# The norm between two transformer blocks: scale at the projection's eviction, raw rows transposed early, residual gain on VectorE

## The reference, cut to what matters

```python
def rms_norm(x, gain):
    xf = x.astype(jnp.float32)
    y = xf * lax.rsqrt(jnp.mean(xf * xf, axis=-1, keepdims=True) + RMS_EPS)
    return (y * gain.astype(jnp.float32)).astype(x.dtype)
...
    h = h + g2 * swiglu(u, ffn_w_gate[layer], ffn_w_up[layer], ffn_w_down[layer])
    return rms_norm(h, final_norm_g)
...
def second_block(x, mem, w_in, w_out, w_mem_kv, ln_g, ln_b, pool_w, pool_scale, w_kv_shared):
    h = x
    for i in range(DEPTH_2):
        if i == N_A_LAYERS:
            k_blocks, v_blocks, k_mean = moba_shared_kv(h, w_kv_shared)
        u = h @ w_in[i]
...
        y = mixed @ w_out[i]
        h = layer_norm(DEEPNORM_ALPHA * h + y, ln_g[i], ln_b[i])
```

## Time and profile before

| | us |
|---|---|
| three runs | 2292.22, 2295.01, 2295.14 |
| median | 2295.01 |
| profiled execution | 2295.28 |
| its span in the trace | 2293.3 |
| PE busy | 2107.2 (92%) |
| DVE busy | 1496.7 (65%) |
| ACT busy | 1062.5 (46%) |
| POOL busy | 113.0 (5%) |

### The profile page before, as it was taken

The page is one execution under the profiler, slowest core; times in us unless marked ns, Lnnn a source line. Parts: engine busy times, 40 slices in busy tenths (PEclk is TensorE's granted clock), DMA queues, the critical chain, the costliest instruction groups (busy, mean ns, idle before and its releaser), DMA issues.

```text
span 2293.3 us, 29996 instructions
## 1 busy us (share of the span) xinstructions
PE 2107.2 (92%) x9820; PEld 1732.6 (76%) x9820; DVE 1496.7 (65%) x2638; ACT 1062.5 (46%) x1931; POOL 113.0 (5%) x188
## 2 busy tenths in 40 slices
PE   5996999997889999999999999799799699999796
PEld 4775888875667887888888887588578488888675
DVE  5997998666998776655556556755245755555466
ACT  3533544464335444445544554445334354554542
POOL 2000000220003000000000000200000300000000
PEclk9998999998999999999999999899899799999998
DMA  9997999434887887666556655466426366664452
GB/s 298 357 345 264 362 365 326 122 93 158 309 296 239 270 260 250 193 191 192 186 192 192 192 189 180 137 193 194 172 90 206 91 187 195 191 196 129 169 210 99
DMA packets 321588, 486.08 MB, mean 212 GB/s; under 512 B 33696, under 2 KB 145536, under 8 KB 320064
## 3 DMA queue, kind: packets, MB, share of 16 engines
q1 hardware_dynamic: 318704, 468.63, 62.3%
q0 software_dynamic: 2768, 15.98, 2.0%
HBM read 465.13 MB, written 2.10 MB: 204 GB/s over the span
## 4 chain that ended last, share of the span: by engine, by line
PE 76%; DVE 11%; issue 6%; SPq 3%; DMA 2%; ACT 2%; POOL 0%; DVEq 0%; POOLq 0%; ACTq 0%
PE ps L468 23%; PE ps L470 23%; PE ps L469 23%; DVE w_lo L401 3%; SPq L840 3%; DVE ada_acc L413 3%; PE ps L724 1%; PE ps L687 1%; PE ps L501 1%; PE ps L671 1%; DMA raw<-in_w_mem_kv 1%; PE ps L1373 1%; ACT w_hi L368 1%; DMA raw<-in_w_out 1%; DVE evac L575 1%
## 5 line engine op out<-in xcount | busy, mean ns | idle before, releaser
L401 DVE TENSOR_TENSOR w_lo<-raw,w_hi 128x512 fp32r<-128x512 f32 (+1 forms) x1328 | 916.3, 702 | 597.7 <-ACT w_hi L368 596.0
L368 ACT ACTIVATE w_hi<-raw 128x512 fp32r<-128x512 f32 (+1 forms) x1328 | 829.5, 629 | 968.2 <-PE ps L470 911.7
L468 PE MATMUL ps<-w_hi,actT 128*128 128x512 f32 x2176 | 865.3, 398 | 55.4 <-DVE actT L582 27.4
L470 PE MATMUL ps<-w_hi,actT 128*128 128x512 f32 x2176 | 852.4, 392 | 0.0
L469 PE MATMUL ps<-w_lo,actT 128*128 128x512 f32 x2176 | 851.8, 391 | 0.0
L468 PEld LDWEIGHTS ps<-w_hi,actT 128*128 128x128 f32 x2176 | 414.1, 190 | 150.6 <-DVE actT L582 35.3
L470 PEld LDWEIGHTS ps<-w_hi,actT 128*128 128x128 f32 x2176 | 413.3, 190 | 87.2
L469 PEld LDWEIGHTS ps<-w_lo,actT 128*128 128x128 f32 x2176 | 414.7, 191 | 84.0 <-issue 1.4
L413 DVE SCALAR_TENSOR_TENSOR ada_acc<-raw,c_col,ada_acc 128x512 f32<-128x512 f32 x360 | 269.8, 749 | 10.1 <-DMA raw<-in_ada_w 2.2
L468 PE MATMUL ps<-w_hi,hidT 128*128 128x512 f32 x352 | 137.7, 391 | 2.8 <-DVE w_lo L401 2.8
L470 PE MATMUL ps<-w_hi,hidT 128*128 128x512 f32 x352 | 137.0, 389 | 0.0
(11 more groups left out here) (224 smaller groups left out, 1214.8 us busy)
## 6 DMA issues: line engine op xcount, KB each, us to landing
raw<-in_w_in SPq DMA_DIRECT2D x216, 512.0 KB, 4.3
raw<-in_ada_w SPq DMA_DIRECT2D x192, 512.0 KB, 5.7
raw<-in_w_out SPq DMA_DIRECT2D x96, 512.0 KB, 5.1
raw<-in_ffn_w_gate SPq DMA_DIRECT2D x176, 256.0 KB, 2.9
raw<-in_ffn_w_up SPq DMA_DIRECT2D x176, 256.0 KB, 3.1
raw<-in_ffn_w_down SPq DMA_DIRECT2D x88, 512.0 KB, 4.2
raw<-in_w_kv_shared SPq DMA_DIRECT2D x48, 512.0 KB, 3.6
raw<-in_w_mem_kv SPq DMA_DIRECT2D x32, 512.0 KB, 6.9
```

Source lines behind the costliest of these rows:

```text
L368: act.activation(w_hi[:, g, 0:w], raw[:, slot_of(st, it), b, 0:w], ACT.Copy).then_inc(hi_ready, 1)
L401: nc.vector.tensor_tensor(w_lo[:, g, 0:w], raw[:, slot, b, 0:w], w_hi[:, g, 0:w].bitcast(f32), ALU.subtract).then_inc(blocks_read, 1)
L468: nc.tensor.matmul(o, hi, w_hi[:, g, 0:w], start=(k == 0), stop=False)
L470: last = nc.tensor.matmul(o, lo, w_hi[:, g, 0:w], start=False, stop=(k == nk - 1))
```

## The change

In four parts:

1. **Scale at the eviction.** `normalise("n3", X)` is gone. The turns of `h0` take the raw rows of `X`; `rinv_x` is applied as ACT's `scale` operand when the finished panels of `in0` and `in0m` are copied out of PSUM (`scaled=True`), behind a wait for `rinv`.
2. **Turns beside `down2`.** Groups 0 to 5 are turned by PE at blocks 8 and 9 of `down2`'s panels 1 to 3 (`turn_h0`), each as soon as its quarter of `X` has been added; `mod` and `low` on DVE and `high` on ACT follow in the first blocks of the panel after. `gated_add` moves from block 8 to block 5. The last panel's add, groups 6 and 7, and `moments` stand in `in0`'s first panel.
3. **Residual of `h0` on DVE.** POOL's two passes are replaced by eight scalar_tensor_tensor of 128x512 (times `rinv_x`, times `gb0`), two each at blocks 3 and 9 of `in0`'s second panel and at block 3 of its third and fifth.
4. **Residual of `h1` on DVE.** POOL's four passes beside `kv` are replaced by eight tensor_tensor on 128x2x512 (gain, then shift behind a semaphore), at the same places of `kv`.

```diff
@@ gpsimd @@
-            def natural(tag, gain_row, shift_row):
-                pool.wait_ge(turned, TURNS[tag] + 8)
-                for t in range(T):
-                    ins = g.tensor_tensor(X[:, t, :], X[:, t, :], gain_row[:, :], ALU.mult)
-                    if shift_row is not None:
-                        chain(ins)
-                        ins = g.tensor_tensor(X[:, t, :], X[:, t, :], shift_row[:, :], ALU.add)
-                    ins.then_inc(S("natural"), 1)
...
-            pool.wait_ge(S("fin_in"), 16)
-            natural("h0", gb0, None)
...
-            pool.wait_ge(S("ln0_in"), 32)
-            natural("h1", gb0, gb1)
@@ tensor @@
-                stage_matmuls(pe, f"down{i}", hidT, lead={
+                def turn_h0(g):
+                    pe.wait_ge(acc_read, 2 + ST["down2"].start[2] + g // 2 + 1)
+                    if g >= 4:
+                        pe.wait_ge(turn_taken, TURNS["h0"] + g - 3)
+                    for b in range(4):
+                        k, t = 2 * g + b // 2, b % 2
+                        last = nc.tensor.transpose(ps[:, 4 + g % 4, b * P:(b + 1) * P], x_block(k, t), ident[:, :])
+                    last.then_inc(turned, 1)
+                def h0_quarter(late):
+                    return lambda p, j: turn_h0(2 * j + late)
+                stage_matmuls(pe, f"down{i}", hidT, hooks={8: h0_quarter(0), 9: h0_quarter(1)} if i == 2 else None, lead={
                     0: lambda: pe.wait_ge(S("hid_taken"), 8 * i + 2 * st.bodies - 1),
                     8: lambda: turn(st.bodies - 1, 1),
                     last_k: lambda: pe.wait_ge(S("hid_taken"), 8 * i + 2 * st.bodies)})
-            lead = turning(pe, "h0", x_block, quarter_ready("h0"))
-            stage_matmuls(pe, "in0", actT, lead=lead)
+            def h0_ready(g):
+                pe.wait_ge(turn_taken, TURNS["h0"] + g + 1)
+            def h0_late(g):
+                turn_h0(g)
+                h0_ready(3)
+            stage_matmuls(pe, "in0", actT, lead={
+                0: lambda: h0_ready(0), 2: lambda: h0_ready(1), 4: lambda: h0_ready(2), 5: lambda: turn_h0(6),
+                6: lambda: h0_late(7), 8: lambda: h0_ready(4), 10: lambda: h0_ready(5),
+                12: lambda: h0_ready(6), 14: lambda: h0_ready(7)})
@@ scalar, stage_copy @@
+                    if scaled:
+                        act.wait_ge(S("rinv"), NORM["n3"])
                     for t in range(T):
                         d = dst(p, j, t)
                         w = width[j] if width else NC
-                        last = a.activation(d, ps[:, bank_of(st, j) + t, 0:w], func[j % 2])
+                        last = a.activation(d, ps[:, bank_of(st, j) + t, 0:w], func[j % 2],
+                                            scale=rinv_x[:, t:t + 1] if scaled else 1.0)
@@ scalar @@
+                high_h0 = high_of(act, "h0", actT)
                 stage_split_hi(act, f"down{i}", lead={4: lambda: gate_act(st.bodies - 1, 1),
-                                                      10: lambda: hid_hi(st.bodies - 1, 1)})
+                                                      10: lambda: hid_hi(st.bodies - 1, 1)},
+                               hooks={1: lambda p, j: high_h0(2 * j - 2) if j else None,
+                                      3: lambda p, j: high_h0(2 * j - 1) if j else None} if i == 2 else None)
...
-            take = stage_copy("in0", u_dst, lead=split_mod_hi(act, "h0", actT, normalise("n3", X)), func=gated, defer=True)
-            stage_copy("in0m", um_dst, "u0_done", func=gated, lead={6: take})
+            take = stage_copy("in0", u_dst, lead={
+                2: lambda: high_h0(4), 3: lambda: high_h0(5), 10: lambda: high_h0(6), 11: lambda: high_h0(7)},
+                func=gated, defer=True, scaled=True)
+            stage_copy("in0m", um_dst, "u0_done", func=gated, lead={6: take}, scaled=True)
@@ vector @@
+            mod_h0, low_h0 = mod_low_of(dve, "h0", actT, columns(cols2, 0), None)
...
+                def h0_turn(step, late):
+                    return lambda p, j: step(2 * j - 2 + late) if j else None
+                add_last = gated_add(f"down{i}", 12 if i < 2 else 5,
                                      lead={6: lambda: up_mul(st.bodies - 1, 1),
-                                           11: lambda: hid_lo(st.bodies - 1, 1)}, defer=i < 2)
-            moments("n3", RMS_EPS, True)
-            stage_split_lo(dve, "in0", lead=split_mod_lo(dve, "h0", actT, columns(cols2, 0), None))
+                                           11: lambda: hid_lo(st.bodies - 1, 1)}, defer=True,
+                                     hooks={0: h0_turn(mod_h0, 0), 2: h0_turn(mod_h0, 1), 3: h0_turn(low_h0, 0),
+                                            4: h0_turn(low_h0, 1)} if i == 2 else {})
+            def natural(tag, gain_row, shift_row, loaded):
+                def quarter(q, nth):
+                    xs = X[:, :, ds(q * NC, NC)]
+                    g4 = gain_row[:, ds(q * NC, NC)].unsqueeze(1).broadcast_to([P, T, NC])
+                    if shift_row is None:
+                        for t in range(T):
+                            ins = v.scalar_tensor_tensor(X[:, t, ds(q * NC, NC)], X[:, t, ds(q * NC, NC)],
+                                                         rinv_x[:, t:t + 1], gain_row[:, ds(q * NC, NC)],
+                                                         ALU.mult, ALU.mult)
+                    else:
+                        v.tensor_tensor(xs, xs, g4, ALU.mult).then_inc(S("natural_gain"), 1)
+                        dve.wait_ge(S("natural_gain"), nth)
+                        ins = v.tensor_tensor(xs, xs, shift_row[:, ds(q * NC, NC)].unsqueeze(1).broadcast_to([P, T, NC]),
+                                              ALU.add)
+                    ins.then_inc(S("natural"), 1)
+                def beside_panel(p, j, late):
+                    if isinstance(p, int) and j == 0:
+                        if not late:
+                            dve.wait_ge(turned, TURNS[tag] + 8)
+                            dve.wait_ge(S(loaded), 16 if shift_row is None else 32)
+                            if shift_row is None:
+                                dve.wait_ge(S("rinv"), NORM["n3"])
+                        quarter(*((2, 2) if late else (0, 1)))
+                    elif j == 1 and not late:
+                        quarter(2 * p + 1, p + 3)
+                return {3: lambda p, j: beside_panel(p, j, False), 9: lambda p, j: beside_panel(p, j, True)}
+            stage_split_lo(dve, "in0", lead={1: lambda: mod_h0(4), 2: lambda: mod_h0(5), 3: lambda: low_h0(4),
+                                             4: lambda: low_h0(5), 5: add_last, 8: lambda: moments("n3", RMS_EPS, True),
+                                             9: lambda: mod_h0(6), 10: lambda: mod_h0(7),
+                                             11: lambda: low_h0(6), 12: lambda: low_h0(7)},
+                           hooks=natural("h0", gb0, None, "fin_in"))
...
-            stage_split_lo(dve, "kv", lead=split_mod_lo(dve, "h1", actT, columns(cols2, 16), columns(cols2, 32)))
+            stage_split_lo(dve, "kv", lead=split_mod_lo(dve, "h1", actT, columns(cols2, 16), columns(cols2, 32)),
+                           hooks=natural("h1", gb0, gb1, "ln0_in"))
```

More of the change, by code:

```diff
@@ L910, in program @@
         NORM = {"n1": 1, "n2": 2, "n3": 3, "l0": 4, "l1": 5}
-        XN = {"u1": 0, "u2": 4, "h0": 8, "h1": 12}
+        XN = {"u1": 0, "u2": 4, "h1": 8}
         def quarter_ready(tag):
@@ L1012, in _ @@
             stage_loads(sp, "in0m", lambda p, j, ch: [((0, NC), blocks2(w_in2[0], 0, ch, 2 * BR + j * NC, NC))])
-            sp.wait_ge(S("natural"), T)
+            sp.wait_ge(S("natural"), 4)
             sp.wait_ge(S("u0_done"), 1)
@@ L1021, in _ @@
             sp.wait_ge(S("u1l_done"), 1)
-            sp.wait_ge(S("natural"), 2 * T)
+            sp.wait_ge(S("natural"), 8)
             gather(sp, [(at_moba, pair_moba), (at_mem[1], pair_mem(1))])
@@ L1183, in _ @@
             pool.dma_start(gb0[:, :], bcast(final_g, D)).then_inc(S("fin_in"), 16)
-            pool.wait_ge(S("fin_in"), 16)
-            natural("h0", gb0, None)
-            pool.wait_ge(S("natural"), T)
+            pool.wait_ge(S("natural"), 4)
             pool.wait_ge(S("u0_done"), 1)
@@ L1396, in stage_copy @@
             def stage_copy(name, dst, flag=None, width=None, lead=None, hooks={}, func=(ACT.Copy, ACT.Copy), defer=False,
-                           at=None):
+                           at=None, scaled=False):
                 st = ST[name]
@@ L1834, in subnorm_scale, with gated_add @@
                 last.then_inc(S("o1_ready"), 1)
-            def gated_add(name, at_k=12, take=None, lead=None, defer=False):
+            mod_h0, low_h0 = mod_low_of(dve, "h0", actT, columns(cols2, 0), None)
+            def gated_add(name, at_k=12, take=None, lead=None, defer=False, hooks={}):
                 st = ST[name]
@@ L1858, in f @@
                         panel_stats(st, p, j, q)
```

(9 more changed lines are left out.)

## The result

| | before | after |
|---|---|---|
| median, us | 2295.07 (2292.22 to 2296.07, 4 runs) | 2256.27 (2253.69 to 2258.02, 4 runs) |
| ratio | | 0.9834, 95% interval 0.9821 to 0.9847 |
| profiled execution | 2295.28, span 2293.3 | 2256.58, span 2254.8 |
| PE busy | 2107.2 (92%) | 2099.4 (93%) |
| DVE busy | 1496.7 | 1485.3 |

The account below looks back on a forecast made before the run. It took PE to bound the kernel, with 76% of the chain that ended last and DVE 11%. Gains of 18.4 and 17.2, together 35.6, took 2295.3 to 2259.7; less 0.3 for the median, 2259.4 us, range 2254 to 2270.

Parts of the forecast that it names:

- Seam and `in0`: From `down2`'s end through `in0`'s first panel: 23.0 us lost, 4.6 of it staying, so a gain of 18.4.
- The lost 23.0: PE time lost before the change: 11.40 us between `down2` and `in0`, 11.61 in `in0`'s first panel.
- eight groups in line: All eight groups of transposes for `in0` now run among PE's matmuls, 0.52 us each, 4.2 us staying.
- 0.4 at `in0`'s block 5: In `in0`'s first panel, the last residual add and 3.1 us of `mod` and `low` cost PE 0.4 us.
- The add finds DVE about as far ahead as before: In `down2`'s third and fourth panels, DVE's spare 3.3 us absorbs 3.1 of new work; waits stay 0.4 each.
- bounds of 13.5 us: DVE's added work at `down2` and `in0` could cost PE between 0 and 3.1 + 3.1 + 3.1 + 4.2 us.
- 1.3 us left: In `kv`'s first panel, small PE waits for `low` 5 and 6, 0.6 + 0.7 us, stay out of 18.5 lost.
- Comes free: In `in0`, ACT's scale at the PSUM copy adds no time, as ACT is busy 42 of 84 us.
- Too far behind: Rival: DVE's work beside `down2` and the last add isn't absorbed, up to 13.5 us on PE; 2264 to 2273, chance 0.12.
- POOL was not the cause: Rival: long DVE instructions in `in0` and `kv` return in another form, only the seam pays 8.9 us; 2286, chance 0.05.
- Slower: Rival: DVE's work at twelve new places stops PE and slows its restart, 4.4 us each, 53 us; 2312, chance 0.02.
- Better still: Rival: transposes cost under 0.52 us, `kv`'s 1.3 doesn't show, adds cost nothing; down to 2255, no separate chance.

Follow-up runs that it names:

- e5: Changed kernel with unread bursts of 4 to 10 statistics instructions on DVE before block 3 of panels of `in1` and `in1m`; 2261.49 us, one execution.
- e2: Kernel before, with only the residual of `h1` moved from POOL to DVE; 2278.12 us, ratio 0.9937.
- the later series: Later runs of the unmodified changed kernel beside the kernel before; medians 2257.57 and 2292.76 us, ratio 0.9842.
- e3: Kernel before, with only the residual of `h0` moved from POOL to DVE, the seam's chain kept; 2283.38 us, ratio 0.9961.
- e4: Changed kernel with useless POOL passes of two inputs, one input or only writes in four panels of `in1`; 2262.36 us, one execution.
- e6: Changed kernel with `down2`'s residual add cut in two, product and sum before block 5, statistics before block 7; 2253.15 us, ratio 0.9827.

## Why the prediction was right, point by point

The forecast was 2259.4 with a range of 2254 to 2270; the median is 2256.3.

**Seam and `in0`: 18.4 predicted, 18.7 measured.** The lost 23.0 went. Of what should stay: eight groups in line at 0.52 each, 4.2. From the rows they cost 0.44 each (the matmul behind a group starts 0.35 later than the group's slot and its successor 0.32 later, against 0.23 twice), 3.5. The estimate carried 0.08 too much; it had divided a panel's whole delay among four groups. Of the 0.4 at `in0`'s block 5, 0.3 is there, and no wait is listed for it: the block's first matmul starts at 1445.84, 0.66 us after the start of group 6's transposes and not 0.35, because the `w_lo` behind the add comes late. With these rows in place of the terms, and 0.2 for the growth of the waits in `down2`, the gain would be 19.0. That 18.4 comes within 0.3 of the measured 18.7 is in part luck. The three waits in `down2` stay, and grew a little:

```profile
PE ps L468 <- DVE w_lo L401: 1.5, 3, 0.5
```

against 1.3. "The add finds DVE about as far ahead as before" was right, and e5, which measured the lead in `in1`, gives the reason: 3.94 - 3.45 = 0.49 is the wait of 0.5. The bounds of 13.5 us were too careful; nothing adds up as long as DVE catches up between pieces.

**`kv`: 17.2 predicted, 17.3 measured** (17.0 in e2 alone). Of the 1.3 us left, the rows have two waits of 0.4 at blocks 10 and 12, as forecast, each with a later successor behind it, 0.67 us from start to start: 1.3.

```profile
1795.97 0.50 PE L468 MATMUL ps<-w_hi,actT 128*128 128x512 f32 x1 [0.41 <-DVE actT L582]
...
1799.39 0.50 PE L468 MATMUL ps<-w_hi,actT 128*128 128x512 f32 x1 [0.40 <-DVE actT L582]
```

**The residual's passes on DVE: nothing predicted, nothing measured.** The pieces in `in0` and in `kv`, all under the lead of 3.45:

```profile
1461.56 1.41 DVE L1924 SCALAR_TENSOR_TENSOR X<-X,rinv_x,gb 128x512 f32<-128x512 f32 x2
...
1805.15 1.22 DVE L1928 TENSOR_TENSOR X<-X,gb 128x1024 f32<-128x1024 f32 x1
1806.40 1.22 DVE L1930 TENSOR_TENSOR X<-X,gb 128x1024 f32<-128x1024 f32 x1
```

PE waits for neither. The rule of the Trainium skill on scalar_tensor_tensor (Vector Engine (DVE) Microarchitecture Reference, "Points that are easy to get wrong") does not hold here, read as twice the 0.64 us of a tensor_tensor: the mean of one is 745 ns, not 1.3 us, as the row of the kernel before had said.

**The scale at the eviction** costs ACT 0.09 us a copy (0.68 against 0.59 without it, 16 of each), 1.4 us over 16, on an engine that is busy half the time. "Comes free" was right for the end of the span, not for ACT.

**The sum: 35.6 predicted, 36.0 at these places, 38.8 in all.** The missing 3 us are not in any term; they lie in unchanged stretches, where the clock above all, one wait for a transfer and a rest that I did not trace made them. In the later series the difference of the medians is 35.2 (33 to 39), which fits the 36.0 of the two places. No term of the sum was off by more than 0.7.

**The rivals.** "Too far behind" assumed that the pieces queue up; e5 and the absence of waits rule it out. "POOL was not the cause" is ruled out by e2 and e3. "Slower" needed 3.0 us lost by PE at each of twelve places; PE loses nothing at the residual's pieces of 1.4 and 2.4 us, and 0.78 at an add of 3.94. "Better still" came in part: the transposes cost 0.44 and not 0.52.

## What to carry to other kernels

Before moving work onto an engine that feeds PE, find out how far it runs ahead: a piece shorter than that lead costs nothing, a longer one costs its excess. Behind a wait of 2.60 us PE ran seven matmuls at the slow clock, another 1.6 us; behind waits of 1.36 (e5) and 2.35 (e4) it ran none; behind 2.52 in the kernel before, a few us behind a longer wait, it ran seven. So cut a long piece in two with the feeding instructions between, as e6 did for 2.6 us. And look beside every long instruction of POOL for DVE rows of the same length: here two places with harmless-looking POOL work cost 26 us by holding up subtractions that have nothing to do with it, and the wait was listed under DVE's name.

## What the runs showed of the hardware that was not expected

- POOL's passes with one input (2.2 us each) stop DVE's two-input instructions as those with two do: seven subtractions in 10.73 us instead of 4.8. Passes that only write, six of 1.81 us, don't.
- A POOL pass of 128x2048 takes 4.9 us on `X` and `gb0`, written back to `X`, and 3.6 to 3.9 in e4, with `gb0` twice, written to `gb1`. Which of the two differences makes it was not tested.
- The number of matmuls at 1.2 GHz after the same standstill varies between executions from 0 to 11, up to 2.2 us, and once the clock fell only after four fast matmuls. Differences of a microsecond or two between single traces in unchanged code mean nothing.
